# A kernel of two transformer blocks: two pieces of the projections placed among the modulation's chunks

## The reference, cut to what matters

```python
mod = (jax.nn.silu(c) @ w_ada[l] + b_ada[l])[:, None, :]
sh1, sc1, gt1, sh2, sc2, gt2 = jnp.split(mod, 6, axis=-1)
xn = rms_norm(h, norm1_g[l]) * (1.0 + sc1) + sh1
proj = xn @ w_in[l]
qm, km, vm, zrw, gate_logits = jnp.split(proj, split_at, axis=-1)
...
zrw = token_shift(zrw, rwkv_mu[l])      # z + (z of the token before - z) * mu
zr, zk, zv, zw, za, zg = jnp.split(zrw, rwkv_split, axis=-1)
...
w = -jax.nn.softplus(-(w0 + jnp.tanh(zw) @ w2)) - 0.5
decay = jnp.exp(-jnp.exp(w.astype(f32)))
a = jax.nn.sigmoid(a0 + za @ a2)
g = jax.nn.sigmoid(zg) @ g2
kk = heads(zk * k_k)                    # then normalized over each head
```

## Time and profile before

| | |
|---|---|
| time, median of 3 runs | 1702.52 us (1702.27 to 1712.75) |
| time of the profiled execution | 1704.61 us |
| its span | 1702.7 us |
| its mean granted TensorE clock | 0.979 |
| busy: PE, DVE, ACT, POOL | 96%, 67%, 48%, 7% of the span |
| HBM traffic | 175 GB/s over the span |

### The profile page before, as it was taken

The page is one execution under the profiler, slowest core; times in us unless marked ns, Lnnn a source line. Parts: engine busy times, 40 slices in busy tenths (PEclk is TensorE's granted clock), DMA queues, the critical chain, the costliest instruction groups (busy, mean ns, idle before and its releaser), DMA issues.

```text
span 1702.7 us, 27227 instructions
## 1 busy us (share of the span) xinstructions
PE 1633.7 (96%) x11462; PEld 1488.2 (87%) x11462; DVE 1135.8 (67%) x1971; ACT 817.4 (48%) x1184; POOL 123.2 (7%) x54
## 2 busy tenths in 40 slices
PE   6999999989999999999999999999999998999998
PEld 4889887889999999998899888888898787999996
DVE  5775856752998899995534676666674564656675
ACT  4645434334454444444434444544434655555663
POOL 0001232002646000000000000000000000000000
PEclk8999999999999999999999999999999998999999
DMA  9534331434555545445655686666655343445331
GB/s 390 210 119 160 130 108 51 149 127 146 199 186 177 186 175 181 159 177 178 242 177 194 217 302 230 214 215 219 256 196 171 127 170 123 168 159 168 131 129 59
DMA packets 48604, 301.08 MB, mean 177 GB/s; under 512 B 5601, under 2 KB 6113, under 8 KB 15970
## 3 DMA queue, kind: packets, MB, share of 16 engines
q1 hardware_dynamic: 43586, 290.81, 48.6%
q10 hardware_dynamic: 4896, 8.54, 1.4%
HBM read 288.71 MB, written 9.44 MB: 175 GB/s over the span
## 4 chain that ended last, share of the span: by engine, by line
PE 86%; DVE 8%; ACT 3%; DMA 1%; issue 1%; SPq 0%; DVEq 0%; ACTq 0%
PE ps L603 85%; DVE WL L1958 2%; DVE ar L1931 2%; ACT ar L1355 1%; DVE ar L1942 1%; ACT WH L1363 1%; DVE ar L1950 0%; DMA vec<-in_vec 0%; DMA ar<-in_in_rkv 0%; DVE ar L2261 0%; PE ps L784 0%; DVE ar L2087 0%; ACT L1355 0%; DVE ar L2053 0%; PE ps L1272 0%
## 5 line engine op out<-in xcount | busy, mean ns | idle before, releaser
L1958 DVE TENSOR_TENSOR WL<-ar,WH 128x1024 fp32r<-128x1024 f32 (+1 forms) x428 | 503.2, 1204 | 329.0 <-ACT WH L1363 327.0
L603 PE MATMUL ps<-RH,WH 128*128 128x256 f32 x2136 | 627.2, 294 | 21.4 <-DVE WL L1958 7.1
L603 PE MATMUL ps<-RL,WH 128*128 128x256 f32 x2136 | 609.8, 285 | 0.0
L603 PE MATMUL ps<-RH,WL 128*128 128x256 f32 x2136 | 609.4, 285 | 0.0
L1363 ACT ACTIVATE WH<-ar 128x1024 fp32r<-128x1024 f32 (+1 forms) x478 | 481.6, 1041 | 258.9 <-PE ps L603 243.4
L603 PEld LDWEIGHTS ps<-RH,WH 128*128 128x128 f32 x2136 | 415.1, 194 | 27.8 <-DVE WL L1958 8.2
L603 PEld LDWEIGHTS ps<-RL,WH 128*128 128x128 f32 x2136 | 415.6, 195 | 0.9 <-issue 0.2
L603 PEld LDWEIGHTS ps<-RH,WL 128*128 128x128 f32 x2136 | 415.1, 194 | 0.0
L603 PE MATMUL ps<-WH,RH 128*128 128x512 f32 (+1 forms) x832 | 325.8, 392 | 7.4 <-DVE RL L2455 4.3
L603 PE MATMUL ps<-WH,RL 128*128 128x512 f32 (+1 forms) x832 | 322.4, 387 | 0.0
L603 PE MATMUL ps<-WL,RH 128*128 128x512 f32 (+1 forms) x832 | 322.3, 387 | 0.0
(11 more groups left out here) (155 smaller groups left out, 941.2 us busy)
## 6 DMA issues: line engine op xcount, KB each, us to landing
ar<-in_u SPq DMA_DIRECT2D x64, 1024.0 KB, 4.9
ar<-in_v SPq DMA_DIRECT2D x64, 1024.0 KB, 4.9
ar<-in_adr SPq DMA_DIRECT2D x16, 1024.0 KB, 5.6
ar<-in_ada SPq DMA_DIRECT2D x8, 1024.0 KB, 12.7
ar<-in_in_g SPq DMA_DIRECT2D x8, 1024.0 KB, 5.0
ar<-in_wq SPq DMA_DIRECT2D x8, 1024.0 KB, 4.8
far_gates<-ar ACTq DMA_DIRECT2D x32, 256.0 KB, 2.1
ar<-far_gates SPq DMA_DIRECT2D x16, 512.0 KB, 3.9
```

The lines of the kernel that those rows point to most:

```text
L603: ins = q.matmul(o, l, r, start=start and i == 0, stop=stop and i == len(pairs) - 1, skip_group_check=skip)
L1958: q.tensor_tensor(l[:, x:z, :], src[:, x:z, :], h[:, x:z, :].bitcast(F32), ALU.subtract).then_inc(*v.up(("lo", n, i)))
```

## The change

in_wag and piece 2 of in_rkv move forward in the list, between chunks of the modulation: ada 0, 1, 2, in_wag, ada 3, 4, in_rkv 2, ada 5, 6, 7, and then in_rkv 3 before the first adr chunks. With that all slots of the first 17 loads change; the 18th and all later ones keep place and slot. The new load order on SP is: X, ada 0, 1, 2, in_wag (slot of ada 0), ada 3, 4, in_rkv 2 (slot of ada 1), ada 5, 6 (slot of ada 2), 7 (slot of in_wag), in_rkv 3 (slot of in_rkv 2), the lora's constants, the wait for sum 7, cwide, adr 0, 1, 2, in_rkv 0, adr 3, 4, in_rkv 1, 4, 5. Before, it was: X, ada 0 to 7, in_wag, in_rkv 2, adr 0, 1, 2, the constants with the wait, in_rkv 3, adr 3, 4, in_rkv 0, 1, 4, 5.

PE multiplies these two pieces tile by tile (`by_tile`, six multiplies of 256 columns each) in an order written out by hand among the chunks and sums of the modulation; they have banks 7 and 6 for themselves, and the ring has six banks meanwhile. GpSimd makes their low halves. ACT makes their high halves at takes placed before the norm's root and after tile 2. DVE makes the low part of tile k right after the modulation of tile k from k = 4 on, and one tile later before that. The dot products get other places in ZDOTS: two steps each after units 5, 9 and 11 and four after unit 7 become four after unit 8 and two after units 10, 12 and 14. By the rule of the feed, the calls for the high and low parts of pieces move too: piece 3 before the shift of in_wag (before: after that of piece 2), piece 0 between the dots of adr 0 and adr 1 (before: ahead of those of adr 3), piece 1 from the unit of piece 3's shift to the unit after it, and piece 4 from after piece 0's shift to before it.

```diff
--- before.py
+++ after.py
@@ -61,7 +61,7 @@
 PLACE = {0: 0, 1: 1, 3: 2, 2: 1}
 
 
-ZDOTS = (0,) * 5 + (2, 0, 4, 0, 2, 0, 2) + (0,) * 16
+ZDOTS = (0,) * 8 + (4, 0, 2, 0, 2, 0, 2) + (0,) * 13
 DOTS = ((0, 0, 0, 2, 0, 0, 0, 2, 0, 2, 0, 2), (0, 2, 0, 0) * 3, (0,) * 16)
 EARLY = 12
 LATE_LOADS = {36: 12, 44: 13, 52: 14, 58: 15}
@@ -82,7 +82,7 @@
 
     dots = iter([x for j in range(EARLY) for x in (("adr", j), None)])
     seq = []
-    for u, x in enumerate(of_chunks("in_wag", (0,)) + of_chunks("in_rkv", KRV)):
+    for u, x in enumerate([None] * 8 + of_chunks("in_rkv", KRV[1:])):
         seq += [x] + [next(dots) for _ in range(ZDOTS[u])]
     units = of_chunks("in_v", range(2)) + [None]
     qk = iter(of_chunks("in_qk", range(4)))
@@ -99,7 +99,8 @@
 
 def chunk_order():
 
-    seq = [("ada", j) for j in range(8)] + front_order()
+    seq = [("ada", j) for j in range(8)]
+    seq = seq[:3] + [("in_wag", 0)] + seq[3:5] + [("in_rkv", KRV[0])] + seq[5:] + front_order()
     for n in ("pm", "pr", "wo", "wq", "sub"):
         seq += [(n, j) for j in range(WEIGHTS[n][2])]
     for n, b in (("u", 0), ("u", 1), ("u", 3), ("v", 1), ("u", 2), ("v", 0), ("v", 2), ("v", 3)):
@@ -471,7 +472,7 @@
 
 def low_on_gpsimd(name, j):
 
-    return name == "in_g" or name == "u" and (j < 8 or 12 <= j < 21)
+    return (name, j) in (("in_wag", 0), ("in_rkv", KRV[0])) or name == "in_g" or name == "u" and (j < 8 or 12 <= j < 21)
 
 
 def split_views(m, n, name, j):
@@ -494,11 +495,12 @@
     return i if size(n) == size(n - NS) else 1
 
 
-def walk(name, feed, each=None, js=None):
+def walk(name, feed, each=None, js=None, taken=False):
 
     kt, nf, nch = WEIGHTS[name]
     for j in range(nch) if js is None else js:
-        feed.take()
+        if not taken:
+            feed.take()
         for _ in range(2 * nf - 1):
             yield
         if each is not None:
@@ -630,6 +632,18 @@
             ins.then_inc(*p.up((name, 0)))
             p.mark(("used", n, k // 4))
             yield
+
+    def by_tile(piece, k):
+
+        (n, h, l, _), b, tile = piece
+        p.wait_ge(*on(("lo", n, k // 4)))
+        p.wait_ge(*on(("xs", "tile", k)))
+        for f in range(2):
+            fs = slice(f * P, (f + 1) * P)
+            ins = mm3(b[:, f * T:(f + 1) * T], [(h[:, k, fs], l[:, k, fs], RH[:, k, :], RL[:, k, :])],
+                      start=k == 0 and f == 0, stop=k == 7 and f == 1, skip=True)
+        ins.then_inc(*p.up(tile))
+        p.mark(("used", n, k // 4))
 
     def proj_steps(name, k0, *need, js=None, of=ring, by=None):
         kt, nf, nch = WEIGHTS[name]
@@ -1008,17 +1022,46 @@
 
     def front():
         p.wait_ge(m.con_load, 16)
+        ring["ids"] = list(range(6))
         ada(0)
         ada(1)
         ada_sum(0)
+        ada(2)
+        wag = take(), give(7, ("in_wag", 0)), ("in_wag", 0)
+        ada_sum(1)
         p.wait_ge(*on("x squares"))
         mm(bank(("norm1",))[:, 0:T], [(ones, m.rs)]).then_inc(*p.up(("norm1",)))
-        for j in range(2, 8):
-            ada(j)
-            ada_sum(j - 1)
+        ada_sum(2)
+        ada(3)
+        ada_sum(3)
+        ada(4)
+        key = ("in_rkv", 2 * KRV[0])
+        rkv = take(), give(6, key), key
+        ada_sum(4)
+        for k in range(3):
+            by_tile(wag, k)
+        ada(5)
+        by_tile(wag, 3)
+        ada_sum(5)
+        by_tile(wag, 4)
+        by_tile(rkv, 0)
+        by_tile(rkv, 1)
+        ada(6)
+        by_tile(wag, 5)
+        by_tile(rkv, 2)
+        by_tile(rkv, 3)
+        ada_sum(6)
+        by_tile(rkv, 4)
+        ada(7)
+        by_tile(wag, 6)
+        by_tile(rkv, 5)
         ada_sum(7)
+        by_tile(rkv, 6)
+        by_tile(wag, 7)
+        by_tile(rkv, 7)
+        ring["ids"], ring["at"] = list(range(7)), 0
         dots = dot_chunks()
-        zs = with_dots(chain(proj_steps("in_wag", 0, by="xs"), proj_steps("in_rkv", 0, js=KRV)), dots)
+        zs = with_dots(chain(iter([None] * 8), proj_steps("in_rkv", 0, js=KRV[1:])), dots)
         some(zs, 8)
         p.wait_ge(m.lora_loads, 80)
         for hf in range(2):
@@ -1462,8 +1505,10 @@
         AC(small[:, 8:16], vc("c", 0, 8), ACT.Sigmoid, "c sigmoid")
         a.wait_ge(m.x_load, 16)
         AC(m.XN, m.X, ACT.Square, "x squared")
-        for j in range(2):
+        for j in range(3):
             ada_rows(j)
+        for _ in range(2):
+            feed.take()
         a.wait_ge(*on(("norm1", "rec")))
         AC(m.rs, m.rs, ACT.Sqrt, "rs")
 
@@ -1472,16 +1517,23 @@
             q.activation(RH[:, k, :], m.XN[:, k, :], ACT.Identity, scale=m.mod[:, 48 + k:49 + k],
                          bias=m.mod[:, k:k + 1]).then_inc(*a.up(("xs", "hi", k)))
 
-        for j in range(2, 7):
-            ada_rows(j)
-            first(j - 2)
+        ada_rows(3)
+        first(0)
+        ada_rows(4)
+        first(1)
+        first(2)
+        for _ in range(3):
+            feed.take()
+        first(3)
+        ada_rows(5)
+        first(4)
         first(5)
+        ada_rows(6)
+        first(6)
         ada_rows(7)
-        first(6)
-        for _ in range(7):
+        first(7)
+        for _ in range(5):
             feed.take()
-        first(7)
-        feed.take()
 
         def shifted(first):
             def each(t, f, n):
@@ -1493,7 +1545,8 @@
             return each
 
         dots = dot_chunks()
-        zs = with_dots(chain(walk("in_wag", feed, shifted(0)), walk("in_rkv", feed, shifted(2), KRV)), dots)
+        zs = with_dots(chain(walk("in_wag", feed, shifted(0), taken=True),
+                             walk("in_rkv", feed, shifted(2), KRV[:1], True), walk("in_rkv", feed, shifted(2), KRV[1:])), dots)
         some(zs, 4)
         a.wait_ge(*on(("z", 0)))
         AC(m.zl[0:64, 0, :], m.zl[0:64, 0, :], ACT.Tanh)
@@ -2058,7 +2111,8 @@
 
         def rest_of_first(k):
             v.wait_ge(*on(("xs", "hi", k)))
-            q.tensor_tensor(RL[:, k, :], m.XM[:, k, :], RH[:, k, :].bitcast(F32), ALU.subtract).then_inc(*v.up(("xs", "half", k // 4)))
+            v.wait_ge(*on(("first", k)))
+            q.tensor_tensor(RL[:, k, :], m.XM[:, k, :], RH[:, k, :].bitcast(F32), ALU.subtract).then_inc(*v.up(("xs", "tile", k)))
 
         for k in range(8):
             t = ("ada sum", k)
@@ -2068,15 +2122,16 @@
                                    ALU.add, ALU.mult).then_inc(*v.up())
             q.tensor_tensor(mod[:, k:k + 1], b[:, 1:2], vc("b_ada", k), ALU.add).then_inc(*v.up(("modulation", k)))
             v.mark(("out", t))
-            TS(m.XM[:, k, :], m.XN[:, k, :], mod[:, 48 + k:49 + k], mod[:, k:k + 1], ALU.mult, ALU.add)
-            if k > 0:
+            TS(m.XM[:, k, :], m.XN[:, k, :], mod[:, 48 + k:49 + k], mod[:, k:k + 1], ALU.mult, ALU.add, ("first", k))
+            if 0 < k < 5:
                 rest_of_first(k - 1)
+            if k >= 4:
+                rest_of_first(k)
         for _ in range(7):
             feed.take()
-        v.wait_ge(*v.last())
-        rest_of_first(7)
         v.mark("xs")
-        feed.take()
+        for _ in range(3):
+            feed.take()
 
         def shifted(first):
             def each(t, f, n):
@@ -2852,7 +2908,7 @@
                 s.wait_ge(*on("sub used"))
             else:
                 s.wait_ge(*on(("lo", SPLIT.index((b_name, b_j)), 1)))
-        if c == CHUNKS.index(("in_rkv", KRV[1])):
+        if c == CHUNKS.index(("adr", 0)):
             for dst, src in ((m.lw[:, 0:512], m.D["w2a2"]), (m.lw[:, 512:1024], m.D["g2"]), (m.con[:, C1A:], m.D["con"][:, C1A:]),
                              (m.sA.bitcast(I32), m.D["pos"]), (m.w0[0:1, :], m.D["w0row"])):
                 q.dma_start(dst, src).then_inc(m.lora_loads, 16)
```

## The result

The changed kernel takes 1720.3 us in the median of its runs (1715.4 to 1735.4); the kernel before, beside it, 1705.0 (1701.9 to 1719.1). The ratio is 1.0102, interval 1.0074 to 1.0130. On 1702.5 that is +17.4 us (12.6 to 22.1) where +12.0 was forecast: inside the range of 1702 to 1722 and just above my own case's 1708 to 1720, but it straddles the bound of 1% on which I had put 82 in 100 for "within". The forecast of 1714.5 stood on the 1702.5 of three runs; the nine runs beside the changed kernel give 1705.0, so 2.5 of the 5.8 between 1714.5 and 1720.3 belong to that starting point.

A forecast was written before the change was run, and what follows sets the result against it. The chain of the first 120 us, PE's only in part, was taken to set the change's effect, through Z and DVE's work to W. Z +3.8 and Z to W +8.2 made +12.0 on 1702.5: 1714.5 us, 80% range 1702 to 1722.

The forecast's parts named there:

- my own case: The main forecast, a median of 1714.5 us with a range of 1708 to 1720, given 60 in 100.
- Part 1: Up to the first modulated tile: DVE's product by the root ends at 25.3, +4.4, of which 2.1 waits for GpSimd.
- Part 2: PE up to in_wag's end: chunks wait behind tiles, last modulation at least 12 us later, in_wag's last tile at 48.1.
- Rival A: Clock stays low: tiles broken up by chunks and sums don't restore 2.4 GHz; +9.6, to 1724; 12 in 100.
- B: Rival, front as intended: last modulation stays near 31 with only its two tiles following; 1702.8; 12 in 100.
- D: Rival: waits push the tiles behind the last modulation, which keeps its place; lora starts as before; 1707.7; 9 in 100.
- C: Rival, faster: B, and DVE finds other cover for Part 5; 1694.6; 7 in 100.
- Part 3: in_wag's end to lora: start at 53.6, +6.7; PE idle 4.8, clock priced at 0, bounds -3.5 and +4.3.
- Z: Event: end of the shift of piece 3, 70.71 us before, forecast at 74.5, +3.8.
- Part 4: Lora's start to Z: 20.9, the wait for piece 0's load gone; Z at 74.5, +3.8.
- Part 5: Z to W: 34.6 instead of 26.4, +8.2, as piece 1's copy is called only after ACT's exponentials.
- W: Event: shift of the last piece, 97.15 us before, forecast near 109; said to move the end one for one.

The follow-up runs named there:

- e4: Changed kernel with the low halves of the two early pieces made on DVE instead of GpSimd; ratio to the kernel before 1.0083.
- e9: Changed kernel with modulation chunks and sums first on PE and ACT, the sixteen tiles of both pieces behind the last sum; ratio to the kernel before 1.0034.
- e3: Changed kernel with 38 needless multiplies filling PE's idle time before the lora; ratio to the kernel before 1.0059.
- e6: Kernel before with only the change's new places for the dot products (ZDOTS), no early pieces; ratio to the kernel before 1.0020.
- e1: Changed kernel with the dot products' places on DVE put nearer to the old ones; ratio to the kernel before 1.0054.
- e2: Kernel before with only the load order changed: piece 0 of in_rkv loaded ahead of adr 3 and 4; ratio to the kernel before 1.0020.
- e5: Changed kernel with the last modulation chunks and sums ahead of all tiles on PE and ACT; ratio to the kernel before 1.0080.
- e8: Kernel before with e2's earlier load of piece 0 and needless multiplies in PE's idle times in the modulation; ratio to the kernel before 1.0009.
- e7: Changed kernel with e1's dot order, e2's load order, e3's needless multiplies and e4's low halves on DVE; ratio to the kernel before 1.0038.
- e10: e9 with e1's dot order and e2's earlier load of piece 0; ratio to the kernel before 1.0006.

## Why the prediction was right or wrong

**Part 1** holds. The product ran from 20.79 to 24.91, +4.0 (predicted +4.4): 1.8 of it beyond its 2.29 is the wait for GpSimd (predicted 2.1, bounds 0 and 2.4). GpSimd's halves ended at 22.76, and the product 2.15 after that: it waited them out, and the flat 1.63 would have been 0.2 short. The copy of in_wag, the table load and the root stand one behind the other as summed, and the root follows the table load's 19.05 and 1.28 at 20.34, without a drain.

**Part 2** holds in its mechanism: the last sum's end is 46.7 (predicted 46.0), and in_wag's last tile ends at 49.1 (48.1). I put the meeting of piece 2's low half with DVE's tiles at 0.4. It took two instructions, 2.38 and 2.58 at 30.70 and 33.00 instead of 0.41 and 0.42, and PE's tile 3 of in_wag waited for them. Part of that lay under a chunk, and e4, without GpSimd, starts the lora only 1.6 sooner. Rival A fell: the clock came back between 34 and 35 us, under chunk 5, whose sixteen PE instructions took 1.50, between the 1.93 of half rate and the 1.07 of full. B and D fell with PE's last chunk at 43.6, and C, which needs B, with them. e9 shows that it was PE's order and not the loads that put it there.

**Part 3** is the step that failed. Its interval was right (in_wag's end to lora 5.5, as predicted; PE idle 4.77, predicted 4.8), and so the lora starts at +7.7 for +6.7, the 1.0 being Part 2's. The clock was priced at 0, with "its clock was at half for most of 50 to 55 anyway". That compared the same microseconds and not the same instructions: in the earlier trace rows the half clock of 50 to 55 fell on the lora's second part, after its first four had run at full. After 4.77 of idle time the clock fell about 0.5 us into the four, so they ran at half as well, and the others no faster (7.04 for their 7.07). Lora to Z took 24.0 where 20.9 was predicted. e3 filled only the idle time: lora to Z 20.8, first four 4.2. The cost of 3.1 to 3.5 lay inside the bound of +4.3; the value chosen was wrong. The Trainium skill (TensorE: Matmul & The Clock Gate, What's actually happening) makes half rate the default and full rate what activity releases. The trace agrees in that the half rate followed the idle gap, and not in the other half: PE was busy from 56 to 68 us at a granted 0.50. In no profile here did all of the lora run at full, the case of -3.5.

**Part 4** otherwise holds: 20.9 from the lora to Z, measured 20.8 in e3 and 20.4 in e9, with piece 0's load no longer waited for.

**Part 5** holds: Z to W 34.9, predicted 34.6, +8.5 for +8.2. Its listed terms add up to +8.4, so most of this 0.3 is a slip in the sum and not in the mechanism. e6 shows it without the early pieces and e1 shows it gone. With the lora's start it makes up most of the loss: the order on DVE is worth 5.6 to 7.6 of settled shift (e6 over before; after over e1), the front 8.6 (after over e6), of which 3.5 is the clock (after over e3). The 1.3 by which e6's lora started sooner than before's belongs to neither; without it the two are some 6.9 and 7.3.

**W against the end.** The sum for W came out 4.3 short (109.2, measured 113.5): 1.0 from Part 2, 3.1 from the clock, 0.3 from Part 5. That W moves the end one for one was too simple. 16.3 at W became 14.3 at 176 us, since in_v no longer stands behind it. After that the distance changes with the granted clock: the profile of before fell to half for some 3.5 us at 764, 948 and 1214 us and that of after did not, which would be some 1.7 lost each time (an estimate: half of each stretch). I can't say from one profile each whether such drops belong to a kernel or to an execution. The medians say +17.4 (12.6 to 22.1), which holds both 14.3 and 16.3.

**What stays open.** In e2, 3.7 sooner at W and to 187 us, the ratio is no gain (1.0020, 0.9992 to 1.0048), so at least 2.3 of it was lost on the way. In its profile the table load of 1065 us stands at 1070.70, 5.3 behind the kernel before, so that execution lost 9.0 between the two marks. It has 27 us in one piece at half clock, from 241 to 268, where before has 7 (windows of e2, and of before):

```profile
240.00:260.00 20.00, 18.96 (x131) 14.17 (x129) 12.15 (x36) 5.95 (x21) 0.94 (x1) 0.52 0.17 54
```

```profile
240.00:260.00 20.00, 16.74 (x175) 12.93 (x173) 14.57 (x42) 7.20 (x24) 2.96 (x2) 0.83 0.15 54
```

That could cost up to 10 (an estimate: half of the 20 us more at half rate), more than e2 had gained, but no run forced the clock there, and e5 and e8 show such stretches too; this cause is argued, not shown. Over the changed kernel and the ten experiments the loss in the runs (the ratio less 1, times 1705) and the settled shift differ by -3.4 (e5) to +7.1 (e2). Open, too, is why equal instructions met another clock before 30 us in e2, e6 and e7: one profile each can't tell a kernel's trait from an execution's.

**The chances.** 82 in 100 for "within 1%" was too much for a forecast of +12.0 with a bound of +4.3 on one term: with that term at its upper end the sum stood at +16.3, on the edge.

## What to carry to other kernels

Work moved ahead on one engine is only worth what it frees on the last input of the next stage: here the products left the end of the stage and the modulation's last chunk took their place, since both wait in one queue; chunks first and tiles behind them (e9) halved the loss. When a queue's order changes, price every order that moves with it (here the dot products behind piece 0 and the copy of piece 1 behind the exponentials cost nearly as much as the front did). An idle gap in front of TensorE's work has a second price, the clock of what follows; compare the same instructions before and after, not the same microseconds. And before a few microseconds between two profiles are called an effect, look whether they were there ahead of the first thing that the edit changes.

## What was not expected of the hardware

- A tensor_scalar on DVE with one SBUF tensor and two per-partition scalars, 128x256 f32, took 2.38 us beside GpSimd's subtraction and 0.41 otherwise. I had taken only two-input operations to be held. The Trainium skill (SBUF — State Buffer, Who interferes with whom) counts tensor_scalar among those that can contend; the trace agrees.
- PE busy without a gap did not bring the clock back: from 56 to 68 us of the changed kernel the lora multiplies ran at a granted 0.50, and in the kernel before and in e3 and e10 the clock fell to half some 4 us after the lora's start, with PE busy (0.59 for 50 to 55 in the earlier trace rows).
- The same chunk (sixteen PE instructions, 128x32 weights) took 1.07 or 1.93 in kernels that had done the same work up to there: at 24.5 us 1.93 in the kernel before, 1.07 in e2 and e6. After a wait of 1.72 for a load the last chunk took 1.94 in e8; after one of 1.20 it took 1.07 in e2.
